# A two-block transformer layer: setup by column halves, the last recurrent chunk and the first attention in another order, block sums by VectorE

## The chip, the cores and the metric

The kernel runs on one core of a Trainium2 chip. The metric is device time in microseconds (us), the median of several executions; the profiled execution is one more, taken by the hardware profiler.

## What is computed

The reference applies two blocks, one after the other, to x of 1024 tokens by 1024 channels, in fp32. What matters here is the first block:

```
c_act = silu(c)
mod = c_act @ w_ada + b_ada                       # 1024 x 6144; six segments of 1024
sh1, sc1, g1, sh2, sc2, g2 = split(mod, 6)
h = rms_norm(x, pre_mix_g) * (1 + sc1) + sh1
y = token_mixer(h, w_in, ...)                     # recurrent heads in chunks, and windowed attention
x = x + g1 * rms_norm(y, post_mix_g)
h = rms_norm(x, pre_ffn_g) * (1 + sc2) + sh2
y = conv_ffn(h, w_up, ffn_conv_w, ffn_conv_b, w_down)
x = x + g2 * rms_norm(y, post_ffn_g)
```

The second block (another attention, a pooling mixer and a gated network) follows and is not touched.

## The kernel before

Activations lie transposed: channels on the 128 partitions, in eight tiles k = 0 to 7 of 128 channels, tokens along the free dimension. Each matrix product is made of three products of rounded parts: a value is split into a high part (fp32r, written by ScalarE) and a low part (the value minus the high part, written by VectorE), and TensorE adds high x high, low x high and high x low. One weight tile against one k and 512 tokens is three matmuls; a weight tile against all k and all 1024 tokens is 48.

**Setup** is a block of its own, and all engines meet at its end. SyncE's queue brings c, then x (two transfers of 2 MB), then 16 row blocks of w_ada for the first two segments (shift and scale; 128 rows by 1024 columns, 512 KB each, numbered n = 0 to 15; eight for each segment), then the first weight tiles into `raw`. TensorE transposes x (`turn`, k by k, into the PSUM tiles `down`), ScalarE copies each k to `xt` and squares it, TensorE adds the squares over the channels with a matmul of ones (`sum_squares`). VectorE multiplies each w_ada row block by its column of silu(c) and adds it to `ada_acc` (`add_ada_row`); after eight of them `reduce_ada` sums over the partitions with eight matmuls of one column. `modulate` and `gains` write `mod` and `coef`. ScalarE makes the first two weight tiles' high parts (`split_hi`), VectorE the low ones (`split_lo`), and ScalarE the root from the sums (`act_rstd`).

**The first norm** (`Norm`, made as `norm_mix`) then runs on three engines in step: for each k VectorE scales (line 534), ScalarE adds the shift and rounds (line 500), VectorE subtracts (line 545). TensorE takes each k as it comes, for the first two weight tiles together (`pair_products`): 12 matmuls for each k, 96 in all. The other tiles of the input projection follow, then the **recurrent chunks** c = 0 to 7 (`chunk_pe`, `chunk_dve`, `chunk_act`, `chunk_pool`): `outputs(c)` and `update(c)` on TensorE into `ps_main`, `ps_update` and `ps_last`; `last_of`, `new_state`, `denominators`, `scale`, `gated` on VectorE; `turn_back(c)` transposes the scaled result.

**The first attention** has 16 units, numbered (n, e) for query block n and key head e. A unit is `scores` on TensorE into `up[e]`, `maxima` on VectorE, `exponentials` on ScalarE, `reciprocals` on VectorE, one product of 128x1024 on POOL (GpSimd, line 1786 of before), `turn` on TensorE, a split into high and low parts, `values`. The function `ahead` of each engine holds what comes before the loop of units, and begins with the chunks' work (`lead.pe`, `lead.dve` and so on).

**The first network** (`ConvFeedForward` over `SplitFeedForward`) multiplies by blocks with seven products instead of eight, and needs sums of operand blocks: `pool_operands(k)` makes four for each k = 0 to 3 on POOL, ScalarE rounds them (`act_sum`), VectorE makes the low parts (`dve_sum`, line 2869). The first four weight tiles are multiplied in the plain way (`pe_quad`), and the network's first pair of tiles by blocks after that, in the order of blocks e = 0, 3, 6, 1, 2, 4, 5. Blocks 1, 2, 4 and 5 use the operand sums.

The order on each engine is the order in which the program is written; engines wait on semaphores.

Of the kernel before, what the change touches and what calls it, by code (L numbers as in the profile page):

```python
# [113 lines left out]
def block_kernel(nc, a, out):  # L114
    ctx = ExitStack()
    with ctx:
# [263 lines left out]
        def pair_products(pe, w, op_lo, u0, after_two=None):  # L380

            for t in range(2):
                pe.wait_ge(up_free, u0 + t + 1)
                pe.wait_ge(lo_done, w + t + 1 + RAW)
            for k in range(DK):
                if k == 2 and after_two:
                    after_two(pe)
                pe.wait_ge(op_lo, k + 1)
                for t in range(2):
                    s = (w + t) % RING  # L390
                    ws = slice(k * P, (k + 1) * P)
                    for hf in range(2):
                        tok = slice(hf * HALF, (hf + 1) * HALF)
                        o = up[t][:, tok]
                        nc.tensor.matmul(o, whi[:, s, ws], hhi[:, k, tok], start=(k == 0), stop=False)
                        nc.tensor.matmul(o, whi[:, s, ws], hlo[:, k, tok], start=False, stop=False)
                        mm = nc.tensor.matmul(o, wlo[:, s, ws], hhi[:, k, tok], start=False, stop=(k == DK - 1))
                    if k == DK - 1:
                        mm.then_inc(used, 1)


        xt = ar(0, DK, T)
        xin = ar(32, NB, D)
        ada_acc = [ar(64, D), chunk_work[:, 7 * D:8 * D]]
        ada_slots = [cbuf[:, i, :] for i in range(2)] + [chunk_work[:, i * D:(i + 1) * D] for i in range(7)]
        ada_slots += [v[:, i * D:(i + 1) * D] for v in (row_hi, row_lo) for i in (2, 3)]
        c_in = lead_work[0:DK, 7 * T:7 * T + P]
        c_turned = up[1][:, 0:DK]
# [11 lines left out]
        squares, x_sums = lead_work[:, :].rearrange("p (k t) -> p k t", t=T), up[0][:, :]  # L420
# [4 lines left out]
        ADA_FIRST = 2  # L425

# [25 lines left out]
        class Norm:  # L452

            def __init__(self, name, src, gain, shift, y=None, y_gain=None, x_in=None, x_back=None, given=None, park=True):
# [12 lines left out]
            def sp(self, sp):  # L471
                if self.park:
                    if self.y is not None:
                        sp.wait_ge(self.x_sum, DK)
                    sp.dma_start(x_park, self.src).then_inc(self.parked, 16)
# [3754 lines left out]
```

## Time and profile before

| | |
|---|---|
| median of 3 executions | 2281.47 us (2278.68 to 2282.75) |
| the profiled execution's own time | 2280.47 us |
| its span, first to last instruction | 2278.7 us |
| TensorE (PE) busy | 2191.4 us, 96% of the span |
| VectorE (DVE) busy | 1615.0 us, 71% |
| ScalarE (ACT) busy | 1122.2 us, 49% |
| GpSimd (POOL) busy | 793.3 us, 35% |

Matmuls overlap, so that a busy TensorE is not one at its peak; the times at which it stands still are what counts. PEld is its weight load. "L534" is line 534 of the kernel.

### The profile page before, as it was taken

The page shows a single profiled execution, that of the slowest core. Times are in us where ns is not written, and L with a number is a line of the kernel's source. Part 1 is how long each engine was busy: PE and PEld are TensorE (multiplying, and loading weights), DVE is VectorE, ACT ScalarE, POOL GpSimd, SP SyncE. Part 2 cuts the span into 40 slices and gives each one's busy share as a digit, 9 for nine tenths or more (in the row PEclk, how much of TensorE's full clock was granted, in tenths as well). Part 3 has the DMA queues.
Part 4 walks back from the last instruction along what each step waited for, and adds up shares of the span by engine and source line. Part 5 has one row for each costly group of instructions (what it writes and reads, how often), then busy time and mean ns, then how long its engine had stood idle before and what let it go on. Part 6 is the DMA issues. An engine that isn't in the chain of part 4 may idle for free.

```text
span 2278.7 us, 28954 instructions
## 1 busy us (share of the span) xinstructions
PE 2191.4 (96%) x10080; PEld 1778.8 (78%) x10080; DVE 1615.0 (71%) x2191; ACT 1122.2 (49%) x1916; POOL 793.3 (35%) x578
## 2 busy tenths in 40 slices
PE   6999998998899999999998999999999999999999
PEld 5888886686688888888876767777778888888887
DVE  6658357727999999985797579993675555556686
ACT  5652257736554444455455578872343333334533
POOL 1120044424623232342022536661364343433310
PEclk9999999999999999999999999999999999999999
DMA  9356532033133232299854230003423333338986
GB/s 353 99 182 221 179 93 65 28 111 130 55 103 120 89 119 90 93 317 387 311 166 141 68 102 20 28 0 130 130 70 102 107 102 107 102 120 318 368 280 230
DMA packets 282782, 332.35 MB, mean 146 GB/s; under 512 B 18626, under 2 KB 180754, under 8 KB 282138
## 3 DMA queue, kind: packets, MB, share of 16 engines
q1 hardware_dynamic: 279976, 323.10, 41.9%
q0 software_dynamic: 2208, 7.37, 0.9%
q8 instruction: 76, 1.25, 0.2%
q14 instruction: 57, 0.46, 0.1%
q10 hardware_dynamic: 465, 0.17, 0.0%
HBM read 251.90 MB, written 79.73 MB: 146 GB/s over the span
## 4 chain that ended last, share of the span: by engine, by line
PE 54%; DVE 9%; POOL 6%; DMA 4%; issue 3%; ACT 3%; SPq 1%; POOLq 0%; DVEq 0%; ACTq 0%
PE ps L2698 11%; PE ps L2699 11%; PE ps L2700 11%; POOL cbuf L1786 4%; DMA shared<-ffn_blocks 3%; PE ps L2724 3%; PE ps L2725 3%; PE ps L2726 3%; PE ps L358 1%; PE ps L360 1%; PE ps L359 1%; DVE wlo L2904 1%; PE ps L326 1%; DVE sum_lo L2907 1%; PE ps L327 1%
## 5 line engine op out<-in xcount | busy, mean ns | idle before, releaser
L2698 PE MATMUL ps<-sum_hi,whi 128*128 128x512 f32 x640 | 249.7, 390 | 1.8 <-DVE cbuf L3419 0.9
L2700 PE MATMUL ps<-sum_hi,wlo 128*128 128x512 f32 x640 | 249.0, 389 | 0.0
L2699 PE MATMUL ps<-sum_lo,whi 128*128 128x512 f32 x640 | 249.0, 389 | 0.0
L2724 PE MATMUL ps<-sum_lo,whi 128*128 128x512 f32 x616 | 240.7, 391 | 0.8 <-ACT arena L2809 0.8
L2726 PE MATMUL ps<-sum_lo,wlo 128*128 128x512 f32 x616 | 239.7, 389 | 0.0
L2725 PE MATMUL ps<-sum_lo,whi 128*128 128x512 f32 x616 | 239.7, 389 | 0.0
L2698 PE MATMUL ps<-hhi,whi 128*128 128x512 f32 x480 | 188.1, 392 | 7.8 <-DVE cbuf L3374 3.3
L2700 PE MATMUL ps<-hhi,wlo 128*128 128x512 f32 x480 | 187.7, 391 | 0.0
L2699 PE MATMUL ps<-hlo,whi 128*128 128x512 f32 x480 | 187.7, 391 | 0.0
L1786 POOL TENSOR_TENSOR cbuf<-cbuf,attn_stats 128x1024 f32<-128x1024 f32 x80 | 151.7, 1896 | 88.2 <-DVE attn_stats L2048 88.2
L796 POOL TENSOR_TENSOR cbuf<-cbuf 128x512 f32<-128x512 f32 (+1 forms) x50 | 77.3, 1548 | 300.8 <-ACT cbuf L783 298.3
L326 PE MATMUL ps<-hhi,whi 128*128 128x512 f32 x416 | 164.6, 396 | 6.4 <-DVE arena L4055 5.0
L327 PE MATMUL ps<-hlo,whi 128*128 128x512 f32 x416 | 163.5, 393 | 0.0
L328 PE MATMUL ps<-hhi,wlo 128*128 128x512 f32 x416 | 163.5, 393 | 0.0
L263 DVE TENSOR_TENSOR wlo<-raw,whi 128x1024 fp32r<-128x1024 f32 x51 | 71.0, 1397 | 126.2 <-ACT whi L251 126.1
L2798 ACT ACTIVATE whi<-arena 128x512 fp32r<-128x512 f32 x116 | 73.4, 633 | 170.6 <-DVE arena L2915 75.4
L2698 PEld LDWEIGHTS ps<-sum_hi,whi 128*128 128x128 f32 x640 | 120.3, 188 | 28.8 <-DVE wlo L2864 2.4
L2700 PEld LDWEIGHTS ps<-sum_hi,wlo 128*128 128x128 f32 x640 | 120.1, 188 | 25.1
L2699 PEld LDWEIGHTS ps<-sum_lo,whi 128*128 128x128 f32 x640 | 120.3, 188 | 24.7
L2724 PEld LDWEIGHTS ps<-sum_lo,whi 128*128 128x128 f32 x616 | 115.6, 188 | 25.2 <-DVE wlo L2904 1.4
L2726 PEld LDWEIGHTS ps<-sum_lo,wlo 128*128 128x128 f32 x616 | 115.6, 188 | 24.1
L2725 PEld LDWEIGHTS ps<-sum_lo,whi 128*128 128x128 f32 x616 | 115.7, 188 | 23.9 <-issue 0.2
(455 smaller groups left out, 5573.9 us busy)
## 6 DMA issues: line engine op xcount, KB each, us to landing
shared<-ffn_blocks SPq DMA_DIRECT2D x154, 256.0 KB, 5.0
lead_work<-in_w_down SPq DMA_DIRECT2D x105, 256.0 KB, 4.4
arena<-in_w_down SPq DMA_DIRECT2D x100, 256.0 KB, 3.8
raw<-in_w_up SPq DMA_DIRECT2D x36, 512.0 KB, 4.8
ffn_blocks<-chunk_work SPq DMA_DIRECT2D x66, 256.0 KB, 2.3
ffn_blocks<-lead_work SPq DMA_DIRECT2D x66, 256.0 KB, 2.3
raw<-in_w_in SPq DMA_DIRECT2D x32, 512.0 KB, 4.7
arena<-in_w_ada SPq DMA_DIRECT2D x32, 512.0 KB, 5.7
```

What stands on the lines that cost most here:

```text
L326: nc.tensor.matmul(acc[:, tok], whi[:, s, ws], hhi[:, k, tok], start=(k == 0), stop=False)
L327: nc.tensor.matmul(acc[:, tok], whi[:, s, ws], hlo[:, k, tok], start=False, stop=False)
L328: mm = nc.tensor.matmul(acc[:, tok], wlo[:, s, ws], hhi[:, k, tok], start=False, stop=(k == DK - 1))
L796: nc.gpsimd.tensor_tensor(total, total, cbuf[:, self.slot(r, k), tok], ALU.add).then_inc(self.added[r], 1)
L1786: nc.gpsimd.tensor_tensor(p, p, st[:, sl, 16:16 + q].unsqueeze(2).to_broadcast([P, q, T // q]), ALU.mult).then_inc(S["scaled"], 1)
L2698: nc.tensor.matmul(o, hi[:, ws], mhi, start=fresh and k == 0, stop=False, skip_group_check=True)
L2699: nc.tensor.matmul(o, hi[:, ws], mlo, start=False, stop=False, skip_group_check=True)
L2700: mm = nc.tensor.matmul(o, lo[:, ws], mhi, start=False, stop=(k == 3), skip_group_check=True)
L2724: nc.tensor.matmul(o, hi[:, ws], mhi, start=fresh, stop=False, skip_group_check=True)
L2725: nc.tensor.matmul(o, hi[:, ws], mlo, start=False, stop=False, skip_group_check=True)
L2726: return nc.tensor.matmul(o, lo[:, ws], mhi, start=False, stop=(u % self.Q == self.Q - 1), skip_group_check=True)
L2798: nc.scalar.activation(self.wh(self.down_slot(u)), self.sums[s], ACT.Copy).then_inc(F["hi"], 1)
```

## The change

1. **Setup.** The 16 w_ada transfers now bring the first 512 columns of both segments (n = 0 to 7), then the second 512 of both (n = 8 to 15), in pieces of 2 KB. TensorE multiplies row blocks 0 to 12 itself, with eight matmuls of one column each (`multiply_ada`); VectorE adds only rows 13 to 15. The sum of squares moves to ScalarE, token by token before the transpose (`accum_out`), and is spread back by one product with the identity and two matmuls. x is copied out of PSUM by VectorE (k 0 to 3) and ScalarE (k 4 to 7). The first four k are scaled by the root in setup (`x_unit`). Setup ends with modulation and gains of the first half; row blocks 8 to 15 and the second half's modulation fall in the norm (`FirstNorm`), between k = 0 and k = 4. The small transfers go to POOL's queue, those of the gates and of tiles 2 and 3 behind the block's end, and the store of x behind the rotary tables.
2. **Last chunk and first attention.** `ps_main` moves to `up[1]`, `ps_update` and `ps_last` to `up[0]`. The scores of unit (0, 0) stand ahead of the transposes of the values and the last two `turn_back`; their maximum stands ahead of `scale(7)`; the first of the mixer's copies by POOL stands behind the product of unit (0, 0).
3. **First network.** The 16 operand sums are made by VectorE (`dve_operands`), two k ahead of the first low parts, one ahead of `dve_first`, one among the low parts.

The diff, cut to its core:

```diff
-        ada_acc = [ar(64, D), chunk_work[:, 7 * D:8 * D]]
+        ada_acc = ar(64, D)
+        mod_sums, params_out = [down[1][:, 0:DK], down[0][:, 0:DK]], down[1][:, HALF:HALF + 384]
+        turned_to = [up[1], down[0], up[0], up[1], down[0], up[1], down[0], up[1]]
+        ADA_PE = 13
+        def multiply_ada(pe, n):
+            sums = mod_sums[n // DK]
+            if n % DK == 0:
+                nc.tensor.matmul(sums, onesF[:, :], zeros, start=True, stop=False)
+            pe.wait_ge(s_ada[n], 16)
+            for j in range(DK):
+                mm = nc.tensor.matmul(sums[:, j:j + 1], ada_slots[n][:, j * P:(j + 1) * P], csil[:, n % DK:n % DK + 1],
+                                      start=False, stop=(n == DK - 1 and j == DK - 1))
+            mm.then_inc(ada_multiplied, 1)
...
+            def pe(self, pe):                                  # class FirstNorm
+                for n in range(DK, DK + 3):
+                    multiply_ada(pe, n)
...
+                for k in range(DK):
+                    if k == 4:
+                        pe.wait_ge(ada_added, DK * 2 - ADA_PE)
+                        for j in range(DK):
+                            mm = nc.tensor.matmul(mod_sums[1][:, j:j + 1], ada_acc[:, j * P:(j + 1) * P],
+                                                  onesF[:, 0:1], start=False, stop=(j == DK - 1))
+                        mm.then_inc(ada_reduced, 1)
+                    pe.wait_ge(self.op_lo, k + 1)
+                    for t in range(2):                         # 12 matmuls
...
+                    if k < ADA_PE - DK - 3:
+                        multiply_ada(pe, DK + 3 + k)
...
+                for k in range(4):                             # FirstNorm, VectorE
+                    value(k)
+                    low(k)
+                    if k >= 1:
+                        add_row(ADA_PE + k - 1)
+                dve.wait_ge(ada_reduced, 1)
+                modulate_half(1).then_inc(mod_ready, 1)
+                dve.wait_ge(mod_ready, 1)
+                gains_half(1).then_inc(mod_ready, 1)
+                dve.wait_ge(mod_ready, 2)
+                for k in range(4, DK + 1):
                     if k < DK:
+                        value(k)
+                    if k > 4:
+                        low(k - 1)
...
-        ps_main = [up[0][:, i * HALF:i * HALF + THREE].rearrange("p (h b) -> p h b", b=VA) for i in range(2)]
-        ps_update = up[1][:, 0:THREE].rearrange("p (h b) -> p h b", b=VA)
+        ps_main = [up[1][:, i * HALF:i * HALF + THREE].rearrange("p (h b) -> p h b", b=VA) for i in range(2)]
+        ps_update = up[0][:, 0:THREE].rearrange("p (h b) -> p h b", b=VA)
...
-            pe.wait_ge(kv_in[1], 16)
-            keys.pe(pe)
-            turn_back(NB - 2)
-            return lambda: turn_back(NB - 1)
+            def values_and_turn():
+                pe.wait_ge(kv_in[1], 16)
+                keys.pe(pe)
+                turn_back(NB - 2)
+                turn_back(NB - 1)
+                pe.wait_ge(c_scaled, NB)
+            return values_and_turn
...
+            first_maxima()
             scale(NB - 1)
             gated(NB - 2)
             gated(NB - 1)
...
                 self.lead.dve(dve)
+                self.dve_operands(dve, 0)
+                self.dve_operands(dve, 1)
                 for i, k in self.T_SPLITS[0:3]:
                     self.dve_sum(dve, i, k)
...
                 self.dve_weight(dve, 2, 3)
+                self.dve_operands(dve, 2)
                 self.dve_first(dve, 0)
                 self.dve_weight(dve, 2, 6)
                 for i, k in self.T_SPLITS[3:6]:
                     self.dve_sum(dve, i, k)
+                self.dve_operands(dve, 3)
```

Three places in the order of instructions show the moves. TensorE in setup, before, where ps0 and ps1 are `up`, ps2 and ps3 are `down`, `lead_work` holds the squares and `arena` x or the row sums:

```order
L631 MATMUL ps3<-identF,arena 128x128 x8
L370 MATMUL ps0<-lead_work,onesF 128x512 x2
L376 MATMUL ps1<-onesF,arena 128x1 x8
L631 MATMUL ps3<-identF,arena 128x128 x8
L370 MATMUL ps0<-lead_work,onesF 128x512 x2
```

and of the change, from the end of setup into the norm:

```order
L630 MATMUL ps2<-identF,arena 128x128 x8
L427 MATMUL ps3<-small,chunk_work 128x1 x8
L630 MATMUL ps1<-identF,arena 128x128 x8
L427 MATMUL ps3<-small,chunk_work 128x1 x24
L572 UNCONDITIONAL_BRANCH
L1944 UNCONDITIONAL_BRANCH
L424 MATMUL ps2<-small,onesF 128x8
L427 MATMUL ps2<-small,cbuf 128x1 x16
L427 MATMUL ps2<-small,row_hi 128x1 x8
L502 MATMUL ps0<-hhi,whi 128x512
```

The sums of squares are gone from TensorE, and matmuls of one column on the w_ada rows stand between the transposes, at setup's end and ahead of the first product (line 502).

VectorE at the end of the chunks, before (the last `denominators` and `scale(6)`, then `gated(5)`, `scale(7)`, `gated(6)` and `gated(7)`):

```order
L1547 RECIPROCAL chunk_work<-chunk_work 128x4
L1554 TENSOR_TENSOR chunk_work<-chunk_work 128x4
L1556 TENSOR_TENSOR chunk_work<-ps0,chunk_work 128x384
L1558 TENSOR_SCALAR chunk_work<-chunk_work 128x128
L1564 TENSOR_TENSOR arena<-ps3,chunk_work 128x4x128
L1554 TENSOR_TENSOR chunk_work<-chunk_work 128x4
L1556 TENSOR_TENSOR chunk_work<-ps0,chunk_work 128x384
L1558 TENSOR_SCALAR chunk_work<-chunk_work 128x128
L1564 TENSOR_TENSOR arena<-ps3,chunk_work 128x4x128 x2
L2072 COPY ps3<-small 128x8
L2073 COPY ps3<-small 128x8
L2031 TENSOR_REDUCE attn_stats<-ps0 128x4
```

and of the change:

```order
L1601 TENSOR_TENSOR arena<-ps3,chunk_work 128x4x128
L2071 TENSOR_REDUCE attn_stats<-ps0 128x4
L2075 SCALAR_TENSOR_TENSOR attn_stats<-attn_stats,small 128x4
L2078 TENSOR_TENSOR attn_stats<-attn_stats,small 128x4
L1591 TENSOR_TENSOR chunk_work<-chunk_work 128x4
L1593 TENSOR_TENSOR chunk_work<-ps1,chunk_work 128x384
L1595 TENSOR_SCALAR chunk_work<-chunk_work 128x128
L1601 TENSOR_TENSOR arena<-ps3,chunk_work 128x4x128 x2
```

The maximum (TENSOR_REDUCE) moved ahead of `scale(7)` and of the last two `gated`.

VectorE at the start of the first network, of the change, from the last low parts of the norm (line 881) on:

```order
L881 TENSOR_TENSOR hlo<-arena,hhi 128x512 x2
L3080 TENSOR_TENSOR arena<-arena 128x512
L3082 TENSOR_TENSOR arena<-arena 128x512
L3084 TENSOR_TENSOR arena<-arena 128x512
L3086 TENSOR_TENSOR arena<-arena 128x512
```

The same four follow again for k = 1, and stand at two later places for k = 2 and 3; before, line 2869 came right behind the low parts.

## Rows read from the trace of the kernel before

**Rows 1.** The page: busy time of each engine, and busy tenths of PE in 40 slices.
```profile
PE 2191.4 (96%) x10080; PEld 1778.8 (78%) x10080; DVE 1615.0 (71%) x2191; ACT 1122.2 (49%) x1916; POOL 793.3 (35%) x578
PE   6999998998899999999998999999999999999999
```

**Rows 2.** Timeline of PE, setup and first product: start, length, engine, line, what, [idle before <-releaser].
```profile
14.57 2.82 PE L631 MATMUL ps<-identF,arena 128*128 128x128 f32 x12 [4.25 <-DMA arena<-in_x]
...
21.45 1.04 PE L631 MATMUL ps<-identF,arena 128*128 128x128 f32 x8
...
39.59 1.84 PE L376 MATMUL ps<-onesF,chunk_work 128*128 128x1 f32 x16
46.24 0.77 PE L395 MATMUL ps<-hhi,whi 128*128 128x512 f32 x1 [4.82 <-DVE hlo L545]
...
70.17 0.39 PE L1052 MATMUL ps<-hhi,gateR 128*128 128x512 f32 x1
```

**Rows 3.** Timeline of DVE, setup and the norm's start.
```profile
26.80 0.75 DVE L433 TENSOR_SCALAR chunk_work<-chunk_work,small 128x1024 f32<-128x1024 f32 x1
...
38.19 1.23 DVE L263 TENSOR_TENSOR wlo<-raw,whi 128x1024 fp32r<-128x1024 f32 x1
...
41.82 0.17 DVE L717 TENSOR_SCALAR small<-small 128x8 f32<-128x8 f32 x1
42.31 2.48 DVE L534 SCALAR_TENSOR_TENSOR cbuf<-arena,coef,cbuf 128x1024 f32<-128x1024 f32 x2 [0.32 <-PEq L554]
44.81 1.28 DVE L545 SCALAR_TENSOR_TENSOR hlo<-cbuf,mod,hhi 128x1024 fp32r<-128x1024 f32 x1
```

**Rows 4.** Timeline of ACT, first copy and first square of x.
```profile
15.73 1.02 ACT L679 ACTIVATE arena<-ps 128x1024 f32<-128x1024 f32 x1 [4.14 <-PE ps L631]
16.78 1.06 ACT L681 ACTIVATE lead_work<-arena 128x1024 f32<-128x1024 f32 x1
```

**Rows 5.** Stretches: length, busy PE, PEld, DVE, ACT, POOL, then PEclk, DMA share, GB/s.
```profile
21.00:31.00 10.00, 10.00 (x49) 6.19 (x48) 9.37 (x10) 7.85 (x8) 0.00 (x0) 1.00 1.03 420
34.00:36.00 2.00, 2.00 (x10) 1.20 (x9) 1.90 (x2) 1.33 (x2) 0.00 (x0) 1.00 1.14 344
43.00:44.00 1.00, 0.00 (x0) 0.00 (x0) 1.00 (x2) 0.37 (x1) 0.00 (x0) 0.91 1.07 291
50.00:51.00 1.00, 1.00 (x4) 0.76 (x4) 1.00 (x1) 1.00 (x1) 0.00 (x0) 0.68 1.06 459
```

**Rows 6.** Timelines of PE, DVE, ACT and POOL, last chunk and first two units.
```profile
350.09 0.60 PE L1487 MATMUL ps<-identF,chunk_work 128*128 128x128 f32 x4
354.44 0.79 PE L1924 MATMUL ps<-bandR,identR 128*128 128x512 f32 x1 [0.95 <-DVE chunk_work L1558]
...
352.02 0.69 DVE L1564 TENSOR_TENSOR arena<-ps,chunk_work 128x512 f32<-128x512 f32 x1
359.14 1.23 DVE L2031 TENSOR_REDUCE attn_stats<-ps 128x4 f32<-128x1024 f32 x1
360.67 1.22 DVE L1676 TENSOR_TENSOR hlo<-ps,hlo 128x1024 fp32r<-128x1024 f32 x1
...
363.25 0.47 ACT L1848 ACTIVATE cbuf<-ps,attn_stats 128x256 f32<-128x256 f32 x1 [0.55 <-DVE attn_stats L2034]
...
363.94 1.89 POOL L1786 TENSOR_TENSOR cbuf<-cbuf,attn_stats 128x1024 f32<-128x1024 f32 x1 [0.31 <-DVE attn_stats L2048]
```

**Rows 7.** DVE groups by form, 566 to 593 us, then two of 593 to 601 us.
```profile
L2869 DVE TENSOR_TENSOR sum_lo<-arena,sum_hi 128x512 fp32r<-128x512 f32 x5 | 8.4, 1719 | 0.2 <-ACT sum_hi L2778 0.2
L856 DVE TENSOR_TENSOR hlo<-arena,hhi 128x512 fp32r<-128x512 f32 x3 | 5.2, 1768 | 0.0
...
L2864 DVE TENSOR_TENSOR wlo<-arena,whi 128x512 fp32r<-128x512 f32 x3 | 2.0, 681 | 0.0
```

**Rows 8.** Timelines of PE and POOL, first network.
```profile
596.29 0.50 PE L2698 MATMUL ps<-sum_hi,whi 128*128 128x512 f32 x1 [0.70 <-DVE wlo L2864]
...
611.64 0.77 PE L2698 MATMUL ps<-hhi,whi 128*128 128x512 f32 x1 [3.31 <-DVE cbuf L3374]
```

More of the change, by code:

```diff
@@ L651, in _, with turn @@
-                pe.wait_ge(par_copied, 1)
-                pe.wait_ge(ada_added, 2 * DK)
-                reduce_ada(up[1], HALF, ada_acc[1]).then_inc(ada_reduced, 1)
+                def turn(k, blocks):
+                    for b in blocks:
+                        mm = nc.tensor.transpose(turned_to[k][:, b * P:(b + 1) * P], xin[:, b, k * P:(k + 1) * P], identF[:, :])
+                    if blocks[-1] == NB - 1:
+                        mm.then_inc(x_turned, 1)
+                for b in range(2):
+                    pe.wait_ge(s_x[b], 16)
+                    for k in range(3):
+                        turn(k, range(4 * b, 4 * b + 4))
@@ new lines, in _ @@
+                pe.wait_ge(sums_zero, 1)
+                pe.wait_ge(c_sig, 2)
+                multiply_ada(pe, 0)
+                pe.wait_ge(x_copied, 1)
+                turn(3, range(NB))
+                multiply_ada(pe, 1)
+                pe.wait_ge(s_par, 16 * n_par)
+                for c in range(3):
+                    mm = nc.tensor.transpose(params_out[:, c * P:(c + 1) * P], par_in[:, c, :], identF[:, :])
+                mm.then_inc(par_turned, 1)
+                pe.wait_ge(x_copied, 2)
@@ new lines, in _ @@
+                turn(4, range(NB))
+                multiply_ada(pe, 2)
+                pe.wait_ge(x_copied, 4)
+                pe.wait_ge(rstd_spread, 1)
+                for hf in range(2):
+                    mm = nc.tensor.matmul(rstd_sums[:, half(hf)], onesF[:, :], rstd_blocks[:, half(hf)], start=True, stop=True)
+                mm.then_inc(x_summed, 1)
+                turn(5, range(NB))
+                multiply_ada(pe, 3)
+                pe.wait_ge(x_copied_late, 1)
+                turn(6, range(NB))
@@ L655, in _ @@
+                multiply_ada(pe, 4)
+                pe.wait_ge(x_copied_late, 2)
+                turn(7, range(NB))
+                for n in range(5, DK):
+                    multiply_ada(pe, n)
             @block.scalar
@@ L677, in _ @@
-                for k in range(DK):
-                    act.wait_ge(x_turned, k + 1)
-                    nc.scalar.activation(xt[:, k, :], down[k % 2][:, :], ACT.Copy).then_inc(x_copied, 1)
-                    act.wait_ge(x_copied, k + 1)
-                    nc.scalar.activation(squares[:, k, :], xt[:, k, :], ACT.Square).then_inc(x_squared, 1)
-                for w in range(AHEAD):
-                    split_hi(act, At(w))
-                act.wait_ge(x_summed, 1)
-                norm_mix.act_rstd(act, 0)
+                nc.scalar.activation(csig, c_turned, ACT.Exp, scale=-1.0).then_inc(c_sig, 1)
@@ L2069, in ahead @@
                     def ahead():
-                        lead.dve(dve)
-                        if not full:
+                        if full:
+                            lead.dve(dve)
+                            maxima(At(0), 0)
+                        else:
+                            lead.dve(dve, lambda: maxima(At(0), 0, (sinks, sinks_in)))
                             nc.vector.tensor_copy(sink_neg, sinks)
```

361 lines of the change are left out of this document (171 added, 190 removed).

## Prediction

> **What bounds the kernel now.** I read the page first: TensorE is busy 96% of the span, and its tenths are below 9 only in the first slice and at a few later ones [rows 1]. A slice is 57 us, so the first one (6 tenths) holds all of setup and the norm's start: that is the largest standstill. VectorE is busy 71%, so time is won only where TensorE waits, and there by what ends its wait. Then I read three places in order of time.
>
> Setup and norm. TensorE starts when x has landed, at 14.57, and has its first product at 46.24, after 4.82 us without work that VectorE's low part ended [rows 2]. Behind x it has little to do: between 21 and 31 VectorE is busy 9.37 of 10 us, and the DMA engines move 420 GB/s [rows 5]. So setup goes by VectorE's row additions and by the transfers that feed them. It ends at 42.31 on VectorE [rows 3]; from there to the first product are 3.93 us. The pair of first tiles, 96 matmuls, fills 46.24 to 70.17 [rows 2]. TensorE's granted clock fell from full speed (2.4 GHz) to half (1.2 GHz) near 43.8, after the last row sums, and came back near 50.6, 4.4 us into the products (mean 0.91 in 43 to 44, 0.68 in 50 to 51 [rows 5]).
>
> Last chunk and first attention. The first scores wait for `scale(7)` and start at 354.44; their maximum starts only at 359.14, behind `gated(7)`; the product of unit (0, 0) on POOL starts at 363.94 and the first exponential of the next unit at 363.25 [rows 6]. The chain goes through VectorE.
>
> First network. From 566 to 593 VectorE's subtractions of 128x512 take 1719 and 1768 ns, and 681 ns once POOL's sums are done [rows 7]; the second block starts at 596.29 behind a weight's low part, and the second pair of tiles at 611.64 after 3.31 us without work [rows 8].
>
> **Setup, until the blocks' barrier.** I take the work of each engine from 14.57 on. VectorE: four copies of 1024 from PSUM at 1.22 (a tensor_tensor of this size from PSUM [rows 6]), the spread root 1.2, parameters 0.5 (an estimate from the same rate for 384 columns), four `x_unit` and two `split_lo` at 1.23 [rows 3], a memset 0.5, modulation and gains three to four times 0.17 [rows 3]: 4.9 + 1.7 + 7.4 + 0.5 + 0.6 = 15.1. It starts after eight transposes, about 15.8 (cold pace, 0.235 each [rows 2]), and waits some 2.4 for `turn(3)` and the root: 33.3. ScalarE: eight squares with sums at 1.06 [rows 4] to 1.25, four copies at 1.02 [rows 4], two `split_hi` and the root, some 3: 32.1. TensorE: 24 transposes until about 20.2, 43 more at 0.13 (21.45: eight in 1.04 [rows 2]), 5.6, eight row blocks of eight one-column matmuls at 0.115 (16 in 1.84 [rows 2]), 7.4, and the spread 0.9: it could end at 34.1, but overlaps VectorE's part, of which only the last row block matters; waits for the transfers come instead. With 512 KB per row block at 420 GB/s [rows 5], 1.25 us, and 1 MB of raw tiles in between, row block 7 lands near 30.4, 1.2 before it is needed. The barrier adds 0.3 [rows 3]. So setup ends near 33.7 instead of 42.3: 8.6 earlier. The first value needs ScalarE 1.1 and VectorE 1.2, with hand-offs 2.8 instead of 3.9; row blocks 8 to 10 on TensorE (24 x 0.115 = 2.8) fill the same time. First product: 36.5 instead of 46.24, 9.7 earlier.
>
> **The norm gives much of it back.** Before, the pair took 23.93, of which the half clock over 4.4 us cost 2.2; at full clock a half of it is 10.9. Now TensorE also carries row blocks 11 and 12 (1.84) and the sum over partitions (0.92). It reaches the sum at 36.5 + 10.9 + 1.8 and ends it at 50.2. Only then modulation and gains (0.5), the value of k = 4 (1.24, half of 2.48 [rows 3]), ScalarE 1.15, the low part 1.28 [rows 3], with hand-offs: the next product at 54.8, a new standstill of 4.6. Before, 4.8 us idle left the clock at half; I take one such loss here too, 2.2, wherever it falls. End of the pair: 54.8 + 10.9 + 2.2 = 67.9 instead of 70.2: **2.3 gained**. Bounds: 0.5 (transfers or squares 1 to 2 late) and 4.5 (no loss of clock). VectorE's three row additions (TENSOR_SCALAR 0.75 [rows 3], two at 1.24) lie beside the products of k = 0 to 3. The moved small transfers cost nothing: the gates and tiles 2 and 3 are wanted after the pair, over 30 us after the barrier, and their queues are otherwise empty; without that cover each would cost its own 1 to 2 us.
>
> A rule of the Trainium skill speaks against part of this. First the rows: they show TensorE at 0.235 per transpose at 14.57 and at 0.13 at 21.45 [rows 2], with hardly anything but transposes between: they did raise its clock. The Trainium skill, "TensorE: Matmul & The Clock Gate", Part 4 (PE-mode transpose), says that the full clock does not engage for transposes, since they do not count as busy in the same way. By the row setup's later transposes cost 0.13 and the gain is 2.3; by the rule it is the second rival below. I go by the row.
>
> **Last chunk and first attention.** The scores no longer wait for VectorE's `scale(7)`; they can stand right behind `turn_back(5)` (350.09 to 350.69 [rows 6]), 3.7 earlier. Their maximum follows `gated(5)` (ends 352.71 [rows 6]) instead of 359.14: 6.4 earlier, for 1.23 and two small operations placed ahead of `scale(7)` and the last `gated`, which nothing on TensorE wants at once. Not all of it is kept: `values` needs the split low part on VectorE (360.67 before [rows 6]), which still stands behind scale, gated(6), gated(7) and the reciprocals and moves by about 1.6 to 2.8 only, since VectorE has the same work without the waits. The next unit's maximum starts near 359.1 and its exponential near 360.6 instead of 363.25: 2.65. POOL's product starts near 359.8 plus, 4 earlier, so it doesn't bind. **2.7 gained**, kept over the units because each is paced by its predecessor. Bounds: 0 (a later unit waits for something else, a weight transfer or POOL) and 4.0 (POOL's 4.1).
>
> **Block sums on VectorE.** Sixteen sums at the undisturbed pace (681 ns [rows 7]) add 10.9. Away go POOL's sums, beside which a subtraction took 1719 to 1768 instead of 681, 1.05 to 1.1 too much each [rows 7]; over VectorE's operations until 593 I count 13.4 of excess (5 x 1.04 and 3 x 1.09 from these rows, 4.9 from a value, three weight parts and a pass over 1024 in the same stretch). Net 2.5 less work, but the first sums now stand ahead of low parts that TensorE needs first, and it has the four plain tiles to chew on meanwhile. The second block starts near 595.2 instead of 596.29: **1.1 gained**, bounds 0 and 2.5. ScalarE's rounding follows the sums and has room (49% busy [rows 1]).
>
> **Sum.** 2.3 + 2.7 + 1.1 = 6.1. The profiled execution took 2280.47, 1.0 below the median of 2281.47. 2280.5 - 6.1 = 2274.4, and on the median's footing 2275.4. What a measurement can tell from no change is 0.2%, 4.6 us: faster means below 2276.9, slower above 2286.0.
>
> **Rivals.**
> First, a larger gain: the one-column matmuls and the spread keep the clock at full through the standstill at k = 4 (4.5 for setup), POOL's start decides in the attention (4.0) and the network gives 2.5: 11.0, 2270.5. For it: setup leaves TensorE never idle for long. Against it: before, the clock fell near 43.8, within 2.4 us of the end of 16 such matmuls at 41.43 [rows 2, 5]. Chance 0.16.
>
> Second, on the other side: setup's TensorE work runs at half clock. Then 43 transposes cost 0.105 more each, 4.5, and 64 one-column matmuls, if they double, 7.4; TensorE becomes setup's last engine and the 2.3 gained turn into 9.6 lost. The total is 9.6 - 3.8 = +5.8, 2287.3. It decides from about half of the setup at half clock. For it: a one-column matmul streams almost nothing, and the longest stretch of them in the rows has 16. Against it: the transposes at 21.45. If the clock falls only in the last part, some 5 us of work at half pace, the setup loses 1.5 instead and the total is -2.3, 2279. Chance 0.19 for the strong form. The rule of the Trainium skill on transposes, above, would give this strong form.
>
> Third, no measurable change: the standstill at k = 4 is longer, or transfers bind. The queue has 1 MB of raw tiles between row blocks 3 and 4, and moved 344 GB/s while they came [rows 5] instead of 420; at that rate (1.5 us each) rows 4 to 7 come 1.6 later, past the 1.2 of slack, and rows 13 to 15, from which the sum at k = 4 is made, later too. Setup then gives 0 to 1; the attention's gain may be taken by a later wait as well. With 1.0 + 1.5 + 0.5 = 3.0: 2278.5. With the milder second rival, chance 0.23.
>
> That leaves 0.42 for the forecast, with a range of its own of 2272 to 2277. Faster 0.58, same 0.23, slower 0.19. For 8 in 10 I go down to 2269, the first rival with a little over its bounds, and up to 2288, which takes in the second rival.
>
> **What the profile after should show.** Setup's barrier near 33.7 and the first product near 36.5; TensorE's clock at full from about 20 on; two row blocks between the first products; a standstill of 4 to 5 us at k = 4, released by VectorE; the first gate product near 68. First scores near 347 to 349 (350.7 less the setup's gain), maximum right behind `gated(5)`, 2 to 3 us less between `turn_back(5)` and the second unit's exponential. VectorE's subtractions in the network near 0.68 while the sums are made, and the second block some 6 us earlier than 596.29. Wrong would be: a mean clock well below 1 in 22 to 34; a product before k = 4 that waits for a DMA; a standstill over 7 us; subtractions still at 1.7.

## The result

| | before | changed |
|---|---|---|
| median | 2282.8 us (6 executions, 2278.7 to 2283.7) | 2308.6 us (6 executions, 2303.4 to 2313.0) |
| ratio | | 1.0114, interval 1.0103 to 1.0125 |
| span of the profiled execution | 2278.7 us | 2309.7 us |

The change makes the kernel 26 us slower (23.5 to 28.5). The forecast was 2275.4, range 2269 to 2288. The second rival, TensorE at half clock in setup, was the nearest, and even its 2287.3 is 21 us short. One execution of a later kernel (attention and network together), of 2543 us, was a slow one and is left out of its ratio.

**Where the time went.** The page of the changed kernel, busy time of each engine, then PE and its granted clock in 40 slices of 58 us:

```profile
PE 2224.5 (96%) x10248; PEld 1817.5 (79%) x10248; DVE 1605.9 (70%) x2207; ACT 1117.0 (48%) x1920; POOL 768.7 (33%) x565
...
PE   7999998999989999999998999999999999999999
...
PEclk8899999999999999999999999999999999999999
```

PE is busier by 33 us and has 168 instructions more [rows 1]. TensorE's share in the first slice is higher than before (7 tenths instead of 6), so it waits less there, and its granted clock is at 8 tenths in the first two slices. The timeline of PE in setup and the norm (start, length, engine, line, what, [idle before <- releaser]):

```profile
16.46 2.82 PE L630 MATMUL ps<-identF,arena 128*128 128x128 f32 x12 [4.37 <-DMA arena<-in_x]
...
19.36 3.55 PE L427 MATMUL ps<-small,chunk_work 128*128 128x1 f32 x16
22.77 1.95 PE L630 MATMUL ps<-identF,arena 128*128 128x128 f32 x8
24.51 3.41 PE L427 MATMUL ps<-small,chunk_work 128*128 128x1 f32 x16
...
33.44 3.76 PE L654 MATMUL ps<-cbuf,onesF 128*128 128x512 f32 x4
36.99 1.31 PE L630 MATMUL ps<-identF,arena 128*128 128x128 f32 x8
38.14 1.84 PE L427 MATMUL ps<-small,chunk_work 128*128 128x1 f32 x16
...
43.36 9.32 PE L427 MATMUL ps<-small,chunk_work 128*128 128x1 f32 x48
...
53.83 6.97 PE L427 MATMUL ps<-small,cbuf 128*128 128x1 f32 x32
...
64.07 0.77 PE L502 MATMUL ps<-hhi,whi 128*128 128x512 f32 x1
...
80.70 1.84 PE L493 MATMUL ps<-onesF,arena 128*128 128x1 f32 x16
86.89 0.79 PE L502 MATMUL ps<-hhi,whi 128*128 128x512 f32 x1 [4.35 <-DVE hlo L539]
...
100.38 0.39 PE L1083 MATMUL ps<-hhi,gateR 128*128 128x512 f32 x1
```

Line 427 is `multiply_ada`. One row block is eight matmuls in the code and sixteen instructions in the trace: an fp32 matmul is issued as two. It takes 3.41 us at the first places (19.36 to 22.77) and 1.70 at 38.14 (to 39.84). There is no standstill in setup between 16.46 and 52.68, when TensorE comes to the barrier; it works all the time, at half pace for most of it. The first product comes at 64.07 instead of 46.24, the first gate product at 100.38 instead of 70.17 [rows 2]: 30.2 us later. The same stretch in windows (length, busy PE, PEld, DVE, ACT, POOL, then PEclk, DMA share, GB/s):

```profile
43.00:53.00 10.00, 9.68 (x53) 9.60 (x51) 1.92 (x5) 1.94 (x2) 0.00 (x0) 0.57 0.34 105
53.00:64.00 11.00, 10.59 (x50) 10.62 (x50) 10.06 (x12) 4.63 (x4) 0.00 (x0) 0.50 0.78 174
```

From 43.36 to 64.07 TensorE does nothing but one-column matmuls, apart from the barrier and a zeroing of eight columns; the clock falls in the first window (0.57) and is at half in the second (0.50, that is 1.2 GHz). VectorE works 1.92 of 10 us before the barrier, and the DMA engines are a third busy. The bound has moved from VectorE and the transfers to TensorE.

**What came back later.** The attention, timelines of DVE, ACT and POOL:

```profile
384.70 1.22 DVE L2071 TENSOR_REDUCE attn_stats<-ps 128x4 f32<-128x1024 f32 x1
...
389.88 1.19 DVE L1714 TENSOR_TENSOR hlo<-ps,hlo 128x1024 fp32r<-128x1024 f32 x1
...
392.43 0.47 ACT L1888 ACTIVATE cbuf<-ps,attn_stats 128x256 f32<-128x256 f32 x1 [4.12 <-DVE attn_stats L2075]
...
391.71 1.89 POOL L1823 TENSOR_TENSOR cbuf<-cbuf,attn_stats 128x1024 f32<-128x1024 f32 x1
```

Against [rows 6] the maximum is 25.6 later, the split 29.2, the second unit's exponential 29.2, POOL's product 27.8. From the later units on the whole kernel is 28.75 behind, 1.45 less than at the first gate product. That difference isn't the attention's. With TensorE's instructions of both traces laid side by side, the changed kernel is only 28.56 behind already at 300 us, ahead of the last chunk. The 1.65 went at one place, in the weight tiles right behind the gates, where TensorE of the kernel before ran at half clock and that of the changed kernel, at the same matmuls, did not (windows of before, then of the changed kernel):

```profile
136.00:138.00 2.00, 2.00 (x7) 1.54 (x6) 1.93 (x3) 0.00 (x0) 0.00 (x0) 0.50 0.89 244
...
166.00:168.00 2.00, 2.00 (x11) 1.64 (x10) 1.93 (x3) 0.00 (x0) 0.00 (x0) 1.00 0.73 215
```

Over the last chunk and the first attention this one trace shows no gain at all, 28.56 to 28.75. What the other traces show there stands below, with the parts alone.

In the network, DVE groups by form, 594 to 622 us (busy, mean ns), then PE's second pair of tiles:

```profile
L2913 DVE TENSOR_TENSOR sum_lo<-arena,sum_hi 128x512 fp32r<-128x512 f32 x7 | 4.5, 685 | 0.0
L3084 DVE TENSOR_TENSOR arena<-arena 128x512 f32<-128x512 f32 x4 | 2.8, 693 | 0.1
...
L881 DVE TENSOR_TENSOR hlo<-arena,hhi 128x512 fp32r<-128x512 f32 x4 | 2.8, 692 | 0.9 <-ACT hhi L898 0.9
```
```profile
639.50 0.76 PE L2742 MATMUL ps<-hhi,whi 128*128 128x512 f32 x1 [3.33 <-DVE cbuf L3431]
```

The subtractions take 685 to 692 ns instead of 1719 and 1768 [rows 7], and the pair is 27.86 behind [rows 8]: 0.9 back. The profiled execution loses 3 us more at scattered places behind 1190 us; the times (26 us) don't hold that part.

### The profile page after: what moved, and what is told of

It is laid out like the page before. It is cut to its first block, busy times and chain, and to the rows that moved or that the text cites. A ratio compares the mean times of both kernels' runs of the same rounds, so it can differ in the third digit from the quotient of the medians.

```text
span 2309.7 us, 29304 instructions
## 1 busy us (share of the span) xinstructions
PE 2224.5 (96%) x10248; PEld 1817.5 (79%) x10248; DVE 1605.9 (70%) x2207; ACT 1117.0 (48%) x1920; POOL 768.7 (33%) x565
## 4 chain that ended last, share of the span: by engine, by line
PE 53%; DVE 9%; POOL 7%; DMA 5%; issue 3%; ACT 3%; SPq 1%; POOLq 0%; DVEq 0%; ACTq 0%
PE ps L2742 11%; PE ps L2744 11%; PE ps L2743 11%; POOL cbuf L1823 4%; PE ps L2768 3%; PE ps L2770 3%; PE ps L2769 3%; DMA shared<-ffn_blocks 3%; PE ps L358 1%; PE ps L360 1%; PE ps L359 1%; PE ps L326 1%; PE ps L327 1%; PE ps L328 1%; DVE sum_lo L2951 1%
```

## The experiments

Ratios are against the kernel before on the same chip. The times of most kernels with the new setup scatter by 10 us and more, so their intervals are wide; where a profile is clearer, it is named.

**The parts alone.** The parts of the diff, applied to the kernel before: setup and norm; attention; network; the last two together.

> The kernel before with only the setup and first norm of the change. Theory A (TensorE's row blocks in setup carry the whole loss; the trace of the changed kernel has its first gate product 30.2 us later, and what follows gives 2.4 back): 27 to 30 us slower than before, about 2311. Theory B (part of the loss comes from the moved chunk or the block sums): less than 24 us slower.

> The kernel before with only the swapped banks and the moved scores and maximum. Theory A (the shift falls from 30.2 at the first gate product to 28.75 in the units of the attention): 1.4 to 2.7 us faster. Theory B: no gain or a loss, because TensorE's last update already stood 31.3 behind.

> The kernel before with only the operand sums made by VectorE. Theory A (shift 28.75 before the network, 27.85 behind its second pair): 0.9 us faster. Theory B (a coincidence of that execution): within 0.4 us of before or slower.

> The kernel before with the second and third part of the change, without the first. Theory A: the gains add, 2.3 to 3.7 us faster than before, about 2279. Theory B: the two share a cover and give less than 1.5 together.

| kernel | ratio | interval | us |
|---|---|---|---|
| setup and norm alone | 1.0145 | 1.0123 to 1.0167 | +33 (28 to 38) |
| attention alone | 0.9986 | 0.9976 to 0.9997 | -3.2 (-5.5 to -0.7) |
| network alone | 0.9993 | 0.9984 to 1.0002 | -1.6 (-3.7 to +0.5) |
| attention and network | 0.9984 | 0.9975 to 0.9993 | -3.7 (-5.7 to -1.6) |

Theory A of the first part holds: it carries the whole loss. Alone it costs even a little more than the 27 to 30 expected; in its profile the clock fell to half already in row block 4, at 41, and the first gate product came at 104.55. The other two parts help; the network's share alone lies within what can be told. (The reason given in two of the expectations, that the attention brought the shift from 30.2 to 28.75, was a wrong reading, as shown above.)

Single profiles can't price the attention, since that stretch varies from execution to execution. Laid beside the kernel before, from ahead of the last chunk (250 to 330 us) to the attention's later units (430 to 520), the fourteen profiles with the changed attention, one for each run of this document that has it, moved by between 3.7 less and 1.0 more, 1.3 less on average. The three without it (setup alone, network alone, and the kernel before with its run broken, below) fell 2.0 to 2.4 further behind, and the kernel before is 0 by definition. The two averages are 2.9 apart. For the network, from there to 650 to 760 us, the fourteen profiles with its change came back by 0.4 to 1.1, and the three others without it (attention alone, setup alone, the run broken) fell behind by 0.0 to 0.5. The last kernel (median 2279.9 beside 2283.3) is the best that was found.

**Two wide or narrow fillers.** Extra matmuls behind each row block 0 to 10 of the changed kernel:

```diff
             mm.then_inc(ada_multiplied, 1)
+            if n < DK + 3:
+                for r in range(4):       # or six transposes of 128x128
+                    nc.tensor.matmul(params_out, identR[:, :], bandR[...][:, 0:384], start=True, stop=True)
```

> The changed kernel with four matmuls of 384 columns (identity and band, into a free part of PSUM, results unused) behind each of row blocks 0 to 10, pure extra work for TensorE. Theory clock (in setup TensorE ran at half clock because one-column matmuls between short runs of transposes do not raise it; about 24 us long): the wide matmuls raise it and setup becomes shorter in spite of the added work, first product near 56 instead of 64, 5 to 11 us faster than the changed kernel. Theory count (the clock plays no part, only the number of instructions does): 11 times 0.65 to 1.3 us more, 7 to 14 us slower than the changed kernel.

> The same with six transposes of 128x128 in place of the four wide matmuls. If transposes raise the clock as the row at 21.45 before suggested: as fast as the kernel with wide ones, 3 to 10 us faster than the changed kernel. If they do not count (the Trainium skill, TensorE: Matmul & The Clock Gate, Part 4): 8 to 15 us slower than the changed kernel, with the half clock over all of setup.

Wide: 1.0118 (1.0101 to 1.0135); transposes: 1.0131 (1.0094 to 1.0167). Neither forecast came in. The times are those of the changed kernel within their intervals, so no cost of the added work can be told, nor a gain. In the profile with transposes the clock stood at full from about 20 to 44 and setup ended at 47.8 in spite of 48 extra transposes; with wide matmuls it rose only at 41, and setup ended at 58.0. The difference lay already in row block 0, ahead of any filler (2.10 against 3.55 us), so these two do not compare transposes with wide matmuls.

**Row blocks back to VectorE.**

```diff
-        ADA_PE = 13
+        ADA_PE = 8
...
-                    if k >= 1:
-                        add_row(ADA_PE + k - 1)
+                for n in range(ADA_PE, 2 * DK):
+                    add_row(n)
```

In a second kernel row blocks 4 to 7 go to VectorE in setup as well, with one sum over partitions by TensorE.

> The changed kernel with all eight row blocks of the second half on VectorE, behind its first four low parts, none on TensorE. Theory count (a row block costs TensorE 1.7 us at full and 3.4 at half clock, twice what was forecast): TensorE is rid of 10.5 us ahead of the first product and 3.4 behind it, VectorE ends its rows near 72, just before TensorE wants them; 9 to 12 us faster than the changed kernel. Rival (VectorE is late with the rows and TensorE waits at k = 4 instead): under 5 us faster.

> As the one before, and row blocks 4 to 7 of the first half on VectorE too; TensorE keeps 0 to 3 and one sum over partitions. Theory count: three row blocks less in setup, 5 at full and 10 us at half clock, so 14 to 20 us faster than the changed kernel and still 5 to 12 slower than the kernel before. Rival (VectorE becomes setup's last engine at once): no more than 3 us better than the kernel with the second half's rows alone.

1.0073 (1.0057 to 1.0090), and 1.0038 (1.0024 to 1.0053): by the middle values 9.4 and 17.4 us less than the changed kernel. Against the second measurement of the changed kernel (1.0099, further below) it would be 5.9 and 13.9. So the count's direction and rough size hold, above both rivals, but not each number. A large piece of what remains of the second kernel's loss stands in its timeline of PE (its profile is of its slowest execution, 2299.4 beside a median of 2293.5):

```profile
67.43 0.39 PE L490 MATMUL ps<-small,onesF 128*128 128x8 f32 x2 [3.68 <-DVE arena L549]
67.67 3.37 PE L492 MATMUL ps<-onesF,arena 128*128 128x1 f32 x16
75.39 0.80 PE L501 MATMUL ps<-hhi,whi 128*128 128x512 f32 x1 [4.34 <-DVE hlo L538]
```

The sum at k = 4 waits for VectorE's last row block, runs at half clock after that wait (3.37 instead of 1.84), and the standstill of 4.34 follows: nearly 12 us between the products of k = 3 and k = 4.

**The small transfers.** They go back to SyncE's queue, behind row block 6.

```diff
-                pool.dma_start(sinks_in, ...)              # and two more
...
+                    if n == 7:
+                        sp.dma_start(sinks_in, ...)        # and two more
```

> The changed kernel with the three small transfers back on SyncE's queue, behind row block 6, and the operation on them behind the low parts. Theory (POOL's three transfers, in flight from 9 to 16, took DMA time from x: 141 to 225 GB/s in 13 to 15 instead of 405 to 430 before, x complete at 16.46 instead of 14.57): x complete near 14.6 and all of setup 1.9 earlier, 1 to 4 us faster than the changed kernel. Rival (the squares or w_ada's pieces of 2 KB slow the transfer of x): x stays at 16.4 and the time does not move.

The changed kernel's windows of 12 to 15 us show what they did:

```profile
12.00:13.00 1.00, 0.09 (x1) 0.00 (x0) 0.00 (x0) 0.91 (x3) 0.00 (x0) 1.00 1.62 322
13.00:14.00 1.00, 0.00 (x0) 0.00 (x0) 0.00 (x0) 1.00 (x2) 0.00 (x0) 1.00 0.70 141
14.00:15.00 1.00, 0.00 (x0) 0.00 (x0) 0.00 (x0) 0.84 (x4) 0.00 (x0) 1.00 0.72 225
```

DMA moved 141 and 225 GB/s in the last two; in the same windows of before it was 405 and 430, and with the transfers moved 384 and 408. The second half of x was then there at 15.10 instead of 16.46:

```profile
15.10 2.82 PE L631 MATMUL ps<-identF,arena 128*128 128x128 f32 x12 [2.61 <-DMA arena<-in_x]
```

So three transfers of 4 KB together cost about 1.4 us. The two later kernels with the same move had x at 14.56 and 15.26, the ten profiles with the transfers on POOL's queue at 16.16 to 17.09. The times, 1.0115 (1.0097 to 1.0133), can't show so little.

**A longer run of transposes, and the earlier sum.**

```diff
+                for r in range(12):
+                    nc.tensor.transpose(params_out[:, ...], onesF[:, :], identF[:, :])
                 multiply_ada(pe, 0)
```
```diff
-                    if k == 4:
+                    if k == 2:
                         pe.wait_ge(ada_added, DK * 2 - ADA_PE)
```

> The changed kernel with twelve transposes of a constant (results unused) once, ahead of row block 0, so that TensorE has 24 in a row behind the second half of x instead of 12. Theory (an unbroken run of transposes raises the clock, as the 23 before did; twelve and then one-column matmuls did not): full clock near 21 in place of 37, 12 extra transposes cost 1.6 to 2.8, row blocks 0 to 2 and what lies between save about 8: setup ends near 47 instead of 53.4, 4 to 7 us faster than the changed kernel. Rival (the rise is not tied to the run of transposes): clock rises near 38 to 41 and the kernel is 1 to 3 us slower.

> The changed kernel with the second half's sum over partitions ahead of k = 2 in place of k = 4. Theory (the standstill of 4.35 at k = 4 is the chain modulation, value, ScalarE, low part behind the sum, and the half clock after it costs 2 more): the chain lies beside the products of k = 2 and 3, the standstill goes, first gate product 5 to 7 us earlier. Rival (VectorE is late with its three row blocks, they ended at 64.97, or the values of k = 4 still come late): a new wait at k = 2, under 2 us gained.

> The kernel with the second half's sum ahead of k = 2, again, beside the changed kernel. Its profile had the first gate product at 94.8 instead of 100.4 from the same first product at 64.0, but its times showed no gain. If the gain is real: 4 to 6 us below the changed kernel on this chip. Rival: nothing, and the profiled gain is given back later or belongs to the profiled execution alone.

With twelve more transposes the clock was at full in row block 0 (1.93 us) and fell again in row block 2; setup ended at 49.8 instead of 53.4, not at the 47 expected. The ratio, 1.0112 (1.0085 to 1.0139), shows none of the 4 to 7 us. The early sum, in its first profile:

```profile
74.95 1.93 PE L493 MATMUL ps<-onesF,arena 128*128 128x1 f32 x16
...
94.79 0.39 PE L1083 MATMUL ps<-hhi,gateR 128*128 128x512 f32 x1
```

From the same first product (64.03 against 64.07) the gate product is 5.6 earlier, 6.9 in its second profile, and TensorE stands still nowhere between. The standstill and its cause, the late sum, are shown. The times don't follow: 1.0121 (1.0102 to 1.0141), then 1.0100 (1.0079 to 1.0120) beside 1.0099 for the changed kernel. Where the 5 us went in the timed executions stays open; with a scatter of 10 us and more their medians hardly resolve it.

**The changed kernel again.**

> The changed kernel itself once more, unaltered, beside the next ones on the same chip. Expected 23 to 29 us slower than before, and half clock from 19 to about 37 in its profile as in four of the five profiles with the same setup; if the clock in setup changes from execution to execution, first gate product 4 to 8 us away from 100.4.

1.0099 (1.0073 to 1.0126), executions from 2295.7 to 2316.7. Its profile differs from the first of the same program:

```profile
16.40 2.82 PE L630 MATMUL ps<-identF,arena 128*128 128x128 f32 x12 [4.42 <-DMA arena<-in_x]
...
19.30 1.99 PE L427 MATMUL ps<-small,chunk_work 128*128 128x1 f32 x16
21.15 1.07 PE L630 MATMUL ps<-identF,arena 128*128 128x128 f32 x8
...
57.74 0.77 PE L502 MATMUL ps<-hhi,whi 128*128 128x512 f32 x1
```

Row block 0 took 1.99 here, 3.55 there; the first product came at 57.74 instead of 64.07, the first gate product at 93.74 instead of 100.38, the end at 2299.3 instead of 2309.7. In this setup the clock comes up, or not, from execution to execution. With twelve transposes ahead of row block 0 it was up in 3 of 11 profiles; with 23 or 24 in a row ahead of other work (the setup of before in four kernels, the twelve extra in two) in 6 of 6. The Trainium skill, "TensorE: Matmul & The Clock Gate", Part 1 (The HAM clock gate), says that the moment of the rise changes from run to run and is not worth fitting; the two profiles agree that it changes, and here a missed rise cost 6.3 us of setup. The earlier end of setup in the profile of the moved small transfers (by 7.6) is therefore mostly this, not the edit: its clock was up in row block 0. So was that of the profile with six transposes behind each row block (earlier by 5.6). Beside this second profile of the changed kernel, where the clock was at half again from row block 1 to 2, that one ended setup 0.7 later with 48 transposes more: its clock stayed up, and what that gave about paid for them.

**The clock held up.** Small transfers on SyncE's queue, the early sum, and six transposes behind each row block 0 to 4, twelve behind 5 to 10.

> The changed kernel with the small transfers on SyncE's queue, the second half's sum ahead of k = 2, and behind each row block 0 to 10 six transposes of a constant (twelve from row block 5 on), results unused. If the clock is what costs beside the count: full clock from about 20 on, setup ends at 46 to 49, first product at 54 to 58, first gate product at 81 to 85, that is 14 to 18 us faster than the changed kernel although TensorE does over a hundred transposes more. If only the count of instructions matters: 8 to 12 us of added work, slower than the kernel with the early sum.

1.0078 (1.0059 to 1.0097), 2300.8 beside 2303.7 for the changed kernel. A window of its profile, then two rows of PE's timeline:

```profile
39.00:56.00 17.00, 17.00 (x153) 16.91 (x151) 7.88 (x11) 5.88 (x6) 0.00 (x0) 1.00 0.19 63
...
59.80 1.84 PE L427 MATMUL ps<-small,cbuf 128*128 128x1 f32 x16
61.50 1.51 PE L434 MATMUL ps<-identF,onesF 128*128 128x128 f32 x12
```

The column of the clock alone proves nothing here, since it shows 1.00 from the trace's start (see the end of this text). The pace does: from 40 on each row block took 1.84, and twelve transposes 1.51. So once up, the clock stayed at full through all row blocks (in the changed kernel it was 0.57 and 0.50 there), with transposes of constants between them. With six behind each row block, in the kernel further up, it had fallen at 44, behind the last transposes of x (38.6). But it didn't come up before 39: the first three row blocks took 3.4 each, the first product came at 65.8 and the first gate product at 94.8, not the 81 to 85 expected. The time is 3 us below the changed kernel's, within the intervals: the clock that was won about paid for the 102 transposes, so this kernel doesn't show how much the clock costs.

**Breaking the run in the kernel before.**

```diff
                 turn(1)
+                for j in range(16):
+                    nc.tensor.matmul(up[1][:, HALF + 384 + j:HALF + 385 + j], onesF[:, :], onesF[:, 0:1], start=True, stop=True)
                 params()
```

> The kernel before with sixteen matmuls of one column (constants, results unused) between its first twelve transposes behind x and the next eleven. Theory (the rise of the clock wants an unbroken run of transposes or wide matmuls): full clock not at 19.9 but 3 us or more later, the later transposes at 0.22 until then; setup's end moves by less than 2 us, since VectorE sets it. Rival (the rise comes by time after TensorE starts, whatever it does): full clock near 20 again.

1.0018 (1.0006 to 1.0031). Timeline of PE:

```profile
14.74 2.82 PE L631 MATMUL ps<-identF,arena 128*128 128x128 f32 x12 [4.34 <-DMA arena<-in_x]
17.36 6.82 PE L644 MATMUL ps<-onesF 128*128 128x1 f32 x32
24.04 0.88 PE L622 MATMUL ps<-identF,arena 128*128 128x128 f32 x3
24.71 1.91 PE L631 MATMUL ps<-identF,arena 128*128 128x128 f32 x8
26.42 2.08 PE L370 MATMUL ps<-lead_work,onesF 128*128 128x512 f32 x4
28.34 1.04 PE L631 MATMUL ps<-identF,arena 128*128 128x128 f32 x8
```

Sixteen matmuls of one column took 6.68 us at half clock, and the clock rose only during the group at 26.42. The same group, with the same 2.08, starts at 19.54 in the kernel before, 6.9 earlier: one-column matmuls had not raised the clock. The second half of the expectation was wrong: the first product came 6.9 later (53.13), not under 2. The inserted work stood ahead of the parameters' transposes, for which VectorE waits behind its fourth row block, and ahead of x's third tile. Setup before hung on TensorE's order as well.

**All known terms at once.** Small transfers moved, twelve extra transposes, row blocks 0 to 3, 8 and 9 on TensorE, the others on VectorE.

> The changed kernel with the small transfers on SyncE's queue, twelve extra transposes ahead of row block 0, row blocks 4 to 7 and 10 to 15 on VectorE, 0 to 3, 8 and 9 on TensorE. By the terms as now measured (a row block 1.7 at full clock, VectorE 1.28, standstill 4.3 at k = 4): setup ends near 38 to 40, first product near 43, sum at k = 4 near 56, first gate product near 73 to 76 instead of 70.2; with the gains of the attention and the network 0 to 3 us slower than the kernel before. Rival (the clock stays at half for part of setup again): 6 to 9 us slower than the kernel before.

1.0041 (1.0026 to 1.0055), +9 us (5.9 to 12.6): the rival. The clock was up for row block 0 and down again from within row block 1 to row block 2; first product 53.4, first gate product 86.3.

## Why the prediction was wrong

**What held.** The attention: 2.7 forecast, 3.2 (0.7 to 5.5) measured alone, and 2.9 between the averages of the profiles. The single step behind the forecast, the second unit's exponential 2.65 earlier, stands in neither trace that was read for it: it is 1.0 less behind than the first gate product in the changed kernel, and with the attention alone it starts at 363.55, 0.3 later than before. So the size held, but how it comes about stays open. The network: 1.1 forecast, 1.6 alone (interval down to a loss of 0.5), 0.9 in the trace, with the subtractions at 0.69 as said, and 0.4 to 1.1 in every profile that has the change. Together 3.8 forecast and 3.7 (1.6 to 5.7) measured; that it is this close is partly luck. The standstill at k = 4: 4.6 forecast, 4.35 measured.

**What failed is the first term, "2.3 gained"** for setup and norm; the first gate product was forecast at 67.9 and stood at 100.4, 32.5 later. Three steps of it failed, and the trace sizes them:

1. "Eight row blocks of eight one-column matmuls at 0.115 (16 in 1.84 [rows 2])". The row counts instructions, and the sixteen are eight matmuls of the code; the order of the kernel before says x8 at that place. One row block costs 1.70 us, not 0.92. Thirteen row blocks and one sum over partitions: 13 x 0.78 + 0.92 = 11.1 us. At full clock, too, TensorE would then have been setup's last engine: eight row blocks add 6.2 to the 34.1 at which the forecast had it end, against VectorE's 33.3. The kernels with fewer row blocks on TensorE fit the size (9.4 and 17.4 us less).
2. The clock, which the text took at full "from about 20 on". In the profiled execution half clock cost, from the starts above: row blocks 0 to 2, 9.97 against 5.1, 4.9; eleven transposes of 27.79 and eight of 22.77, 2.0; the spread 1.8; row blocks 5 to 7, 4.1; 8 to 10 and their zeroing, 5.1; the first products 2.0. Sum 19.9. The second rival had this mechanism with 0.19; it priced it from the halved row block, and left out row blocks 8 to 10. The size is that of one execution: another of the same program lost 6.3 less up to the first product.
3. "The moved small transfers cost nothing". The reason given speaks only of those behind the block's end. Those of POOL's queue came in the middle of x: 1.9 in the trace, of which their removal gave 1.4 back.

11.1 + 19.9 + 1.9 = 32.9 for the 32.5. That it closes so well is partly luck, since the forecast also erred the other way: it counted 24 transposes at half pace from x's second half on, where twelve of them belong to the first half and are done near 10, and the row at 16.46 has the other twelve. That is 2.8 too much (12 x 0.235), and smaller terms make up for it, such as the spread of the root (1.7 at full clock, 0.9 forecast) and the 0.73 at the barrier.

The step before these had already gone astray: "Behind x it has little to do". [Rows 5] show TensorE busy 10.00 of 10 us between 21 and 31. Much of that does go with the change, the sums of squares of line 370 (the same window of before, that line's instructions alone):

```profile
21.00:31.00 10.00, 7.16 (x17) 2.57 (x16) 1.00 1.03 420
```

But what comes in their place filled it again even by the wrong price: the forecast's own sum had TensorE end at 34.1 and VectorE at 33.3. There was no slack that could hide an error in the price.

**The rule on transposes.** The Trainium skill, "TensorE: Matmul & The Clock Gate", Part 4, has them not count for the full clock. The runs disagree where the run is long: 23 or 24 in a row were followed by full clock in 6 of 6 profiles, and in the kernel with the clock held up they kept it there. After twelve it was not up in 8 of 11. The forecast took the trace's side from a run of 23 and applied it to a sequence of twelve and eight with one-column matmuls between, which is where it failed.

## What to carry to other kernels

Before work is moved to an engine, hold the trace's count of instructions against the code's count of operations: an fp32 matmul is two instructions here, and a price per instruction is half a price per matmul. Look at the receiving engine's busy share in just that stretch, not over the span, and take off what the change removes there. Before a shift between two traces is credited to an edit, look where along the trace it changes. TensorE's clock belongs to the price: one-column matmuls pay double in the stretch they fill, and what follows them pays too.

## What the runs showed of the hardware that was not expected

- A one-column fp32 matmul of 128x128 weights costs 0.21 us at full and 0.43 at half clock (eight in 1.70 and 3.41), twice a transpose of 128x128 (from start to start 0.11 and 0.22). TensorE was without a pause from 43.36 to 52.68 and its clock still fell to half.
- The same program on the same input ran setup at different clocks from execution to execution (first product 57.74 or 64.07, each in one profile), and its times scatter over 21 us, where those of the kernel before scatter over 10.
- The column PEclk shows 1.00 up to the first fall that a trace records, though the pace there can be that of half clock (in the changed kernel a row block in 3.28 us between 24.51 and 27.79). One of the prediction's signs of being wrong, "a mean clock well below 1 in 22 to 34", could therefore not be read off the column. The pace of a known instruction tells the clock there:

```profile
22.00:34.00 12.00, 12.00 (x57) 11.92 (x57) 2.92 (x3) 1.02 (x1) 0.00 (x0) 1.00 1.06 397
```

- The stretch of the last chunk and the first attention, the same instructions in fourteen profiles, varied by 4.7 us against the kernel before.
- Beside three small transfers from POOL's queue, 4 KB in all, the DMA engines moved 141 and 225 GB/s in two windows of a microsecond, and 384 and 408 without them.
